# Gathering tokens for an expert by matmuls that write the transposed columns

## What is computed

```python
xb = xt[tok]                                   # tokens gathered, xt is RMSNorm(h)
gu = xb @ w_gate_up[e] + b_gate_up[e]          # 1024 -> 2048
gate, up = jnp.split(gu, 2, axis=-1)
gate = jnp.minimum(gate, SWIGLU_LIMIT)
up = jnp.clip(up, -SWIGLU_LIMIT, SWIGLU_LIMIT)
hmid = (up + 1.0) * (gate * jax.nn.sigmoid(SWIGLU_ALPHA * gate))
return hmid @ w_down[e] + b_down[e]            # 1024 -> 1024, scaled by the gate and added to the token
```

## Time and profile before

| | us |
|---|---|
| three runs, median | 1203.18 |
| the profiled execution's own time | 1202.36 |
| its span | 1200.6 |
| TensorE busy (matmul) | 1165.7 (97%) |
| VectorE busy | 302.0 (25%) |
| ACT busy | 214.7 (18%) |
| L1559, up matmuls | 464.8 |
| L1583, down matmuls | 233.9 |
| L1524, scatter | 67.6 |
| L1508, gather | 64.3 |
| DMA rate in most slices after 300 us | 413 to 438 GB/s |

### The profile page before, as it was taken

The page is one execution under the profiler, slowest core; times in us unless marked ns, Lnnn a source line. Parts: engine busy times, 40 slices in busy tenths (PEclk is TensorE's granted clock), DMA queues, the critical chain, the costliest instruction groups (busy, mean ns, idle before and its releaser), DMA issues.

```text
span 1200.6 us, 14108 instructions
## 1 busy us (share of the span) xinstructions
PE 1165.7 (97%) x5359; PEld 492.7 (41%) x5359; DVE 302.0 (25%) x680; ACT 214.7 (18%) x404; POOL 6.6 (1%) x13
## 2 busy tenths in 40 slices
PE   9999999999999999999999999999999999999996
PEld 4476556854333333333333333333333333333332
DVE  3456543246221111111211111111111121111112
ACT  2120551221111111111111111111111111112112
POOL 0000010000000000000000000000000000000000
PEclk9999999999999999999999999999999999999999
DMA  9800279338999999999999999999999999999994
GB/s 359 363 1 1 105 273 343 155 141 316 424 427 427 427 433 430 426 438 427 431 430 432 430 427 432 435 427 432 413 427 435 432 430 429 426 426 429 428 423 180
DMA packets 32019, 440.28 MB, mean 367 GB/s; under 512 B 4832, under 2 KB 5088, under 8 KB 13952
## 3 DMA queue, kind: packets, MB, share of 16 engines
q1 hardware_dynamic: 31104, 439.32, 86.9%
q10 hardware_dynamic: 864, 0.19, 0.1%
HBM read 438.45 MB, written 1.05 MB: 366 GB/s over the span
## 4 chain that ended last, share of the span: by engine, by line
PE 85%; DMA 11%; ACT 2%; DVE 1%; issue 1%; POOLq 0%; ACTq 0%
PE quad L1559 33%; PE quad L1583 17%; DMA ring<-in_w_gate_up 11%; PE y_banks L1524 5%; PE quad L1508 4%; PE y_banks L1343 2%; PE y_banks L1157 2%; PE quad L1157 2%; PE quad L1516 2%; ACT work L641 2%; PE y_banks L1179 1%; PE y_banks L1249 1%; PE y_banks L1320 1%; PE quad L1328 1%; PE quad L1454 1%; PE y_banks L1454 1%
## 5 line engine op out<-in xcount | busy, mean ns | idle before, releaser
L1559 PE MATMUL quad<-ring,work 128*64 128x512 f32 x2112 | 464.8, 598 | 7.0 <-DMA ring<-in_w_gate_up 6.7
L1559 PEld LDWEIGHTS quad<-ring,work 128*64 128x64 f32 x2112 | 150.6, 138 | 298.6 <-issue 286.4
L1583 PE MATMUL quad<-ring,work 128*64 128x512 f32 x1056 | 233.9, 595 | 10.9 <-ACT work L641 10.9
L1583 PEld LDWEIGHTS quad<-ring,work 128*64 128x64 f32 x1056 | 87.3, 137 | 144.3 <-issue 118.4
L1098 DVE TENSOR_SCALAR work<-quad 128x512 f32<-128x512 f32 x33 | 22.8, 691 | 307.7 <-PE quad L1559 307.7
L637 ACT ACTIVATE work<-work 128x512 f32<-128x512 f32 x33 | 20.8, 630 | 438.7 <-DVE work L1098 438.7
L1013 DVE CAST work<-cst 96x64 bf16 (+1 forms) x34 | 6.5, 191 | 278.6 <-PE quad L1559 278.6
L1524 PE MATMUL y_banks<-work 64*128 64x512 f32 x272 | 67.6, 615 | 0.7 <-ACT work L647 0.7
L1508 PE MATMUL quad<-h,work 128*64 128x512 f32 x272 | 64.3, 593 | 0.0
L645 ACT ACTIVATE work<-quad 128x512 f32<-128x512 f32 x33 | 19.7, 597 | 243.3 <-PE quad L1583 243.3
L637 ACT ACT_TABLE_LOAD x33 | 42.3, 1283 | 1.1 <-issue 0.5
(11 more groups left out here) (269 smaller groups left out, 824.1 us busy)
## 6 DMA issues: line engine op xcount, KB each, us to landing
ring<-in_w_gate_up SPq DMA_DIRECT2D x37, 4096.0 KB, 32.5
ring<-in_w_gate_up SPq DMA_DIRECT2D x52, 2048.0 KB, 23.0
ring<-in_w_down SPq DMA_DIRECT2D x18, 4096.0 KB, 31.4
ring<-in_w_down SPq DMA_DIRECT2D x25, 2048.0 KB, 21.9
ring<-in_w_mkv SPq DMA_DIRECT2D x8, 1024.0 KB, 23.6
ring<-in_w_in SPq DMA_DIRECT2D x7, 976.0 KB, 17.0
ring<-in_w_down SPq DMA_DIRECT2D x12, 512.0 KB, 10.7
ring<-in_w_o SPq DMA_DIRECT2D x1, 4096.0 KB, 13.0
```

The costliest lines, as they stand in the source:

```text
L1559: ins = mm(bank[n // 2][lo:lo + BLK, :], xgT[:, k % 4 * P + k // 4 * BLK:k % 4 * P + k // 4 * BLK + BLK], up_rows(j, k)[:, n * 512:(n + 1) ...
L1583: ins = mm(bank[3][n * BLK:(n + 1) * BLK, :], lhs, down_rows(j, f)[:, n * 512:(n + 1) * 512], start=(f == 0), stop=(f == KC - 1))
```

## The change

The roles of the operands are exchanged in the gather. A 128 x 128 piece of `h` (128 tokens, 128 columns of the model) is the weights, and the one-hot `pick`, 64 columns, moves. What comes out are 128 model columns by 64 tokens, already transposed. For each of the eight pieces k two matmuls (the two halves t of the tokens) accumulate into their own 64 columns of bank 2. `gathered_columns`, its four transposes, ACT's `gathered_copy` and the buffer `xg_s` are gone. `gathered_out` on VectorE reads bank 2 and waits for `gathered`. Since bank 2 now holds the gathered columns until then, the hidden rows are transposed into bank 3, and TensorE's wait for `xg_ready` moves from the down matmuls to the `gtok` transposes.

```diff
-            def gather(w):
-
-                for t in range(TT):
-                    pe.wait_ge(S["pick_ready"], w * TT + (t + 1))
-                    for n in range(2):
-                        ins = mm(bank[2][n * BLK:(n + 1) * BLK, :], pick[:, t, :], h[:, t, n * 512:(n + 1) * 512],
+            def gather(first=False):
+
+                for k in range(KC):
+                    lo = k % 4 * P + k // 4 * BLK
+                    for t in range(TT):
+                        if first and k == 0:
+                            pe.wait_ge(S["pick_ready"], t + 1)
+                        ins = mm(bank[2][:, lo:lo + BLK], h[:, t, k * P:(k + 1) * P], pick[:, t, :],
                                  start=(t == 0), stop=(t == TT - 1))
                 ins.then_inc(S["gathered"], 1)
-
-            def gathered_columns(w):
-
-                pe.wait_ge(S["xg_copied"], w + 1)
-                for c in range(4):
-                    ins = pe.transpose(bank[3][:, c * P:(c + 1) * P], xg_s[:, c * P:(c + 1) * P], ident)
-                ins.then_inc(S["xgT_mm"], 1)
...
                 pe.wait_ge(S["gsel_ready"], w + 1)
-                gather(w + 1)
+                pe.wait_ge(S["pick_ready"], w * TT + 2 * TT)
+                gather()
                 pe.wait_ge(S["out_copied"], w + 1)
                 scatter().then_inc(S["scattered"], 1)
-                gathered_columns(w + 1)
                 pe.wait_ge(S["hmid_ready"], w + 1)
                 for c in range(4):
-                    ins = pe.transpose(bank[2][:, c * P:(c + 1) * P], h_s[:, c * P:(c + 1) * P], ident)
+                    ins = pe.transpose(bank[3][:, c * P:(c + 1) * P], h_s[:, c * P:(c + 1) * P], ident)
                 ins.then_inc(S["hid_mm"], 1)
                 biases(w + 1)
                 pe.wait_ge(S["hid_ready"], w + 1)
-                pe.wait_ge(S["xg_ready"], w + 3)
...
                 pe.wait_ge(S["gtok_ready"], w + 1)
+                pe.wait_ge(S["xg_ready"], w + 3)
...
-            def gathered_copy(w):
-
-                act.wait_ge(S["gathered"], w + 1)
-                act.activation(xg_s, bank[2][:, :], ACT.Copy).then_inc(S["xg_copied"], 1)
...
-                dve.wait_ge(S["xgT_mm"], w + 1)
+                dve.wait_ge(S["gathered"], w + 1)
...
-                                      bank[3][:, :].rearrange("p (c n s) -> p c n s", c=4, n=2)[:, i:i + m, :, :],
+                                      bank[2][:, :].rearrange("p (c n s) -> p c n s", c=4, n=2)[:, i:i + m, :, :],
```

More of the change, by code:

```diff
@@ L209, in encoder_kernel @@
         kT96 = spl(pair_area(2048, HEADS * SEQ), HEADS)
-        gate_s, up_s, sig_s, xg_s = (pair_area(512 * i, 512) for i in range(4))
+        gate_s, up_s, sig_s = (pair_area(512 * i, 512) for i in range(3))
         h_s = up_s
@@ L257, in encoder_kernel @@
             om_mm om_ready wm_mm h2_ready h2_sq h3T_mm h3T_ready rt_mm
-            xg_copied xgT_mm mask_ready rank_mm gate_in gate_e gates_ready gtT_mm gtT_ready counts_ready
+            mask_ready rank_mm gate_in gate_e gates_ready gtT_mm gtT_ready counts_ready
             chunks_used parts_used gathered xg_ready scattered hid_mm hid_ready out_copied gsel_mm gsel_ready
@@ L628, in _ @@
                 act.activation(ex[:, t, :], lg[:, t, :], ACT.Exp, bias=nmax0[:, t:t + 1]).then_inc(S["gate_e"], 1)
-            gathered_copy(0)
             act.wait_ge(S["gtT_mm"], 1)
-            act.activation(gT[0:NE, :], bank[2][0:NE, 0:SEQ], ACT.Copy).then_inc(S["gtT_ready"], 1)
+            act.activation(gT[0:NE, :], bank[3][0:NE, 0:SEQ], ACT.Copy).then_inc(S["gtT_ready"], 1)
             act.wait_ge(S["counts_ready"], 1)
@@ L637, in _ @@
                 act.activation(sig_s, gate_s, ACT.Sigmoid, scale=ALPHA).then_inc(S["sig_ready"], 1)
-                gathered_copy(w + 1)
                 act.wait_ge(S["hid_mm"], w + 1)
-                act.activation(hT, bank[2][:, :], ACT.Copy).then_inc(S["hid_ready"], 1)
+                act.activation(hT, bank[3][:, :], ACT.Copy).then_inc(S["hid_ready"], 1)
                 act.wait_ge(S["chunks_used"], w * NCH + NCH)
@@ L1598, in _ @@
             residual_in(1, 1)
-            gather(0)
+            gather(first=True)
             pe.wait_ge(S["counts_ready"], 1)
             first = pe.value_load(first_i[0:1, :], min_val=1, max_val=NITEM - 1)
-            gathered_columns(0)
             pe.wait_ge(S["gates_ready"], 2)
             for t in range(TT):
-                ins = pe.transpose(bank[2][0:NE, t * P:(t + 1) * P], gates_e[:, t, :], ident)
+                ins = pe.transpose(bank[3][0:NE, t * P:(t + 1) * P], gates_e[:, t, :], ident)
             ins.then_inc(S["gtT_mm"], 1)
```

## The result

The changed kernel took 1239.31 us (median of 4 runs, 1236.18 to 1240.24) against 1203.78 us before on the same chip (4 runs): ratio 1.0293, 95% interval 1.028 to 1.0306. It is slower by 35.5 us. The forecast was 1246.5 us, a growth of 43.7; the profiled execution, 1239.42 us against 1202.36, grew by 37.1.

The account below looks back on a forecast made before the run. TensorE's 26.87 us per item was taken as the bound, with transfers (29.3 us an expert) also near the limit. 33 x 1.57 = 51.8, + 0.4, - 8.5 gave +43.7 us on 1202.4; forecast 1246.5 us, 8-in-10 range 1239 to 1275.

Parts of the forecast that it names:

- step 4: Off TensorE's path: ACT's lost copy and VectorE's changes give nothing; the wait between ACT's copy and down matmuls stays.
- step 6: Whole loop: longer items stay below the transfers' 29.3 us, so DMA waits and a slow block vanish, giving back 8.5 us.
- Step 1: Per item: removing eight gather passes (1.72 us) and four transposes (0.44 us) saves 2.16 us.
- step 3: Entering the gather's 128-wide weights from 64-wide ones costs a change of shape, 0.15 us per item.
- Step 2: New gather: 32 passes per item, paced by weight loads at 0.112 us, add 3.58 us.
- B: Gather: load and moving columns add, +2.44 us per item, 1275 us in all; chance 0.05.
- D: Gather: loads run ahead, only the 64 columns count, -0.28 us per item, about 1199 us; chance 0.04.
- Step 5: First item: the removed ACT copy and transposes pay for most of the longer gather, leaving +0.4 us.
- Rival C: Whole loop: the transfers hide TensorE's growth, time stays at 1203 us; chance 0.03.
- Rival A: Gather: the clock falls, in every second item 1273 us, in every item 1299 us; chance 0.12.

Follow-up runs that it names:

- the bf16 run: Changed kernel with 32 bf16 matmuls of ones (128 x 128 weights, 64 moving columns) in the gather's place, tokens not gathered: 1200.26 us, ratio 0.997.
- the run with the old gather in the new frame: Changed kernel with the old gather (pick as weights, h moving), still without ACT's copy and the four transposes: 1198.47 us, ratio 0.9961.

## Why the prediction was right

The direction, the mechanism and the place were right; the size was 6.6 us too large on 43.7. Of that, 6.3 us are one term, the wait of step 4. Two smaller misses of the other steps nearly cancel, and that is luck: the change gave back 1.1 us more than step 6 had, and 0.9 us were lost ahead of the experts, where no step looked.

Step 1 (what is saved) and step 3 (the changes of shape) held: the scatter's change of shape did move to the hidden transposes (0.60), and entering the gather cost 0.13 where I had 0.15.

Step 2, which carries the sum, held. The count of 32 passes is in the page, the pace of 0.112 us in the doubled gather, and the rule "the longer of load and moving side" in the chain pieces with 32, 64 and 128 columns, which also settle rivals B and D. B would have made the piece 0.86 us longer with 64 columns than with 32, and it grew by 0.02; D would have made it 1.73 us with 64. No run narrowed the weights, so that it is the load and no other fixed cost of such a pass rests on its rows (the loads of L1503 cover 124.0 of the 128.6 us), and on the bf16 run.

Step 4 is the one that was mis-sized. It said that the wait behind ACT's copy "stays as it is". It fell by 0.19 us in every item, 33 x 0.19 = 6.3 us. I had asked only when the condition of the moved wait is met. What mattered were the instructions, the one that the wait needs and the ring slot's, which stood between `hid_ready` and the first weight load. Putting the line back brought the 0.19 back to the hundredth, in the period (28.25 to 28.44).

Step 5 (+0.4) measured +0.37. Step 6 (8.5 us given back): from the first up matmul to the end of the last down matmul the kernel before needs 1188.8 - 287.2 = 901.6 us, of which 33 x 26.87 = 886.7 are periods and 3.6 + 1.7 the down biases and the slow block behind; 9.6 us are left, most of which hang on transfers (6.7 of waits, 1.5 of a slow block, small ones). The kernel after needs 1225.9 - 288.5 = 937.3 us, 33 x 28.25 = 932.1 and 5.2, with nothing left. (The last item ends 0.3 us short of a period in both kernels, so the differences stand.) So 9.6 was given back, all there was. The account of the profiled execution: + 33 x 1.375 = 45.4 in the loop, + 0.4, - 9.6, and + 0.9 by which the gather began later than before (283.88 against 282.96), in stages that the change does not touch: 37.1 us.

Rival C failed because TensorE had 9.6 us to give back and no more, though the transfers look saturated in both profiles. The run with the old gather in the new frame shows the other side of it: on a shorter item the same transfers swallow 16 of 21 us. One kernel, two slopes: past those 9.6 us a microsecond more on TensorE costs a microsecond, while of a microsecond less two fifths are left (1.9 of 4.6), a fifth (4.7 of 21), or a tenth (3.6 of the 40 that the bf16 passes save, 33 x 1.20). The first of these is the least sure, with 1.1 to 3.2 for the 1.9.

Rival A was closer than it looks: it did not happen at 64 columns, not even with two gathers on end, and did at 32. What decides it was not found; no width between the two was run. Nor was a gather whose `h` is really split in two bf16 parts written; its passes were only priced, and with the transfers as floor it could give this kernel hardly more than the 1200 us of that run.

## What to carry to other kernels

Count executed passes, not lines of code: an f32 matmul was two in these traces, each with its own load of weights, and with 128 columns of weights and few columns moving the load was the price. Here the wide operand as weights cost 3.71 us a gather in f32, in place of some 2.2. The same count of bf16 matmuls took 1.04 us, though a gather that computes with them was not written. Read both slopes at the start: how much idle time a slower engine could fill, and which stream a faster one runs into. And put waits whose value is computed in a register ahead of the wait that ends last, not behind it: in the kernel before that alone took the gap from 0.24 to 0.10 us.

## What the runs showed of the hardware

With 128 x 128 weights an f32 pass took 0.112 us at 1, 32 and 64 moving columns, and not noticeably more at 128 (0.45/4 for transposes, 3.77/32 with the change of shape for the gather). The Trainium skill, "TensorE: Matmul & The Clock Gate", section "LDWEIGHTS (loading the stationary operand)", has the load grow with the weights' columns, 107 ns for 128. For f32 the traces agree.

In bf16 a pass with the same 128 columns of weights took 0.03 us, so its load takes no more than that, less than a third of that rule. The Trainium skill, in the section "Weight-path perf modes — Fast Weight Load (FWL) and DoubleRow" of the same page, has a faster load for 128 columns of any type but f32, by about two. The pace measured here is better by 3.7 against f32, with weights of ones, and the measurement decides.

The clock fell from 1.00 (2.4 GHz) to 0.50 (1.2 GHz) without any wait, in stretches in which the trace calls TensorE fully busy, behind or near the end of 3.7 us of passes that move 32 columns (17 stretches for 34 gathers). It did not after 3.7 us of passes that move 64 or 128, nor after 7.3 us with 64. The only other fall without a wait, up to TensorE's last matmul, came with the down biases, 3.7 us of passes that fill 32 of the 128 rows, and only in six of the nine profiles. It did not come with the wait put back, nor with 32 or 128 moving columns in the gather.
